# Solving the mixers' triangular systems on 64x64 diagonal blocks in two quadrants of TensorE

## The reference

```python
a = jnp.where(strict, jnp.einsum('bhntd,bhnsd->bhnts', kb, k) * decay, 0.0)
t_inv = lax.linalg.triangular_solve(a + eye, jnp.broadcast_to(eye, a.shape),
                                    left_side=True, lower=True, unit_diagonal=True)
u = jnp.einsum('bhnts,bhnsv->bhntv', t_inv, v * beta[..., None])
w = jnp.einsum('bhnts,bhnsd->bhntd', t_inv, kb * jnp.exp(gc)[..., None])
```

## Time and profile before

| | |
|---|---|
| median of 3 runs | 1672.39 us (1670.04 to 1673.32) |
| the profiled execution: its own time | 1669.19 us |
| its span, first to last instruction | 1667.4 us |
| TensorE products busy | 1611.3 us, 97% |
| VectorE busy | 1213.8 us, 73% |
| ScalarE busy | 986.9 us, 59% |
| mean granted clock of TensorE | 0.99 |

### The profile page before, as it was taken

How to read it: one execution, slowest core, us unless ns; L and a number is a source line. 1 busy time by engine, 2 the same in 40 slices (tenths; PEclk the granted TensorE clock), 3 DMA queues, 4 the chain that set the end, 5 groups by cost and what they waited for, 6 DMA issues and landing times.

```text
span 1667.4 us, 29382 instructions
## 1 busy us (share of the span) xinstructions
PE 1611.3 (97%) x12534; PEld 1523.0 (91%) x12534; DVE 1213.8 (73%) x1705; ACT 986.9 (59%) x1486; POOL 0.7 (0%) x6
## 2 busy tenths in 40 slices
PE   8999899999999999899999999989999999899998
PEld 7999899999989999899999988865999988699997
DVE  7889736777748789746777757666788758688864
ACT  7775555556546774565565543347677645567753
POOL 0000000000000000000000000000000000000000
PEclk9999999999999999999999999989999999999999
DMA  7422125455554412126555553620455544055551
GB/s 274 171 77 77 51 77 202 164 194 200 177 199 148 150 63 77 51 76 217 189 181 190 186 180 122 227 76 2 175 179 181 199 176 159 1 204 192 185 192 61
DMA packets 35843, 246.04 MB, mean 148 GB/s; under 512 B 4096, under 2 KB 4480, under 8 KB 6656
## 3 DMA queue, kind: packets, MB, share of 16 engines
q1 hardware_dynamic: 35712, 244.15, 41.2%
HBM read 243.09 MB, written 1.05 MB: 146 GB/s over the span
## 4 chain that ended last, share of the span: by engine, by line
PE 82%; DVE 10%; ACT 6%; DMA 1%; issue 1%; SPq 0%; DVEq 0%; ACTq 0%
PE PS L395 81%; DVE SB L1761 2%; DVE WL L1752 2%; DVE SB L1752 2%; ACT WH L1109 1%; ACT SB L1106 1%; DVE SA L1752 1%; DVE SB L2005 1%; ACT SA L1618 1%; ACT SB L1109 1%; DVE SB L2009 1%; DMA RAW<-w_in 0%; DVE SA L1919 0%; ACT SB L1690 0%; DVE SA L1761 0%
## 5 line engine op out<-in xcount | busy, mean ns | idle before, releaser
L395 PE MATMUL PS<-XH,WH 128*128 128x256 f32 (+1 forms) x2536 | 715.3, 282 | 8.9 <-DVE WL L1752 4.9
L395 PE MATMUL PS<-XL,WH 128*128 128x256 f32 (+1 forms) x2536 | 713.3, 281 | 0.0
L395 PE MATMUL PS<-XH,WL 128*128 128x256 f32 (+1 forms) x2536 | 712.8, 281 | 0.0
L1109 ACT CAST WH<-RAW 128x2048 fp32r<-128x2048 f32 (+1 forms) x229 | 427.0, 1865 | 398.3 <-PE PS L395 363.2
L1752 DVE TENSOR_TENSOR WL<-RAW,WH 128x2048 fp32r<-128x2048 f32 (+1 forms) x229 | 511.3, 2234 | 126.4 <-ACT WH L1109 122.4
L395 PEld LDWEIGHTS PS<-XH,WH 128*128 128x128 f32 (+1 forms) x2536 | 477.6, 188 | 14.6 <-issue 5.7
L395 PEld LDWEIGHTS PS<-XL,WH 128*128 128x128 f32 (+1 forms) x2536 | 475.7, 188 | 2.7 <-issue 1.9
L395 PEld LDWEIGHTS PS<-XH,WL 128*128 128x128 f32 (+1 forms) x2536 | 475.3, 187 | 0.4
L395 PE MATMUL PS<-INHL,WH 128*128 128x512 f32 (+1 forms) x1216 | 334.5, 344 | 1.2 <-DVE INHL L1752 1.2
L395 PE MATMUL PS<-INHL,WL 128*128 128x256 f32 x960 | 269.9, 281 | 0.0
L395 PEld LDWEIGHTS PS<-INHL,WH 128*128 128x128 f32 x1216 | 210.2, 188 | 29.2 <-ACT INHL L1109 1.5
(11 more groups left out here) (144 smaller groups left out, 1409.7 us busy)
## 6 DMA issues: line engine op xcount, KB each, us to landing
RAW<-w_in SPq DMA_DIRECT2D x51, 1024.0 KB, 4.8
RAW<-w_up SPq DMA_DIRECT2D x44, 1024.0 KB, 4.8
RAW<-f_in SPq DMA_DIRECT2D x44, 1024.0 KB, 4.7
RAW<-w_down SPq DMA_DIRECT2D x22, 1024.0 KB, 4.8
RAW<-f_out SPq DMA_DIRECT2D x22, 1024.0 KB, 4.7
RAW<-a_w_in SPq DMA_DIRECT2D x10, 1024.0 KB, 4.8
RAW<-w_out SPq DMA_DIRECT2D x8, 1024.0 KB, 4.8
RAW<-w_bdn SPq DMA_DIRECT2D x4, 1024.0 KB, 4.8
```

What stands on the lines that cost most here:

```text
L395: return e.matmul(out, l, r, start=start, stop=stop, skip_group_check=True)
L1109: e.copy(out, x).then_inc(*A.up(*key, of=of))
```

## The change

The 16 matrices of a mixer are kept for levels 1 to 5 as their diagonal blocks of 64x64 alone: XIc and XTc have 2 directions x 8 matrices of 64 columns, the upper block on partitions 0 to 63 (b = 0) and the lower one on partitions 64 to 127 (b = 1). A product of the two upper or the two lower blocks takes a quadrant of the array; b = 0 and b = 1 are issued in turn, into two banks of PSUM. The groups are now two (one for a direction) with 8 products for each b. ScalarE and VectorE read each bank on its 64 partitions, so there are still four copies of Y and four masked copies a level, and two transposes in place of four. Level 5 copies corners of 32x256. Level 6 computes the off-diagonal block alone (dn_y6, dn_z6: in the quadrants off the diagonal, one for each direction); ScalarE copies the diagonal blocks (blocks_out) and that block into XTF, full 128x128 matrices, whose fourth quarter GpSimd has set to zero. w_solve reads XTF.

The order changes too: Y of level 1 stands ahead of hg_diag on TensorE and ScalarE; ScalarE's exponential for step 0 stays first; on VectorE hg_mul(1) stands ahead of both placements of level 1; in all levels the placements of both directions stand together, between the first and the second HGRN step (TensorE: Z of both directions between hg_mm(n) and hg_mm(n + 1)).

The diff, cut to its core:

```diff
+        XIc, XTc = SB[:, 6144:7168], SB[:, 8192:9216]
+        XTF = [x.rearrange("p (m n) -> p m n", m=8) for x in (SA[:, 1024:2048], SB[:, 9216:10240])]
+        HALF = (slice(0, 64), slice(64, 128))
...
+                def dn_y(d, lv):
                     w.wait_ge(*V["at", st])
-                    side_placed(g4, lv - 1, 0)
-                    for h in range(4):
-                        last = mm(p[:, h * 128:h * 128 + 128], at_d(g4 // 2, g4 % 2)[:, h], XIv[:, g4, h], True, True)
-                    last.then_inc(*P.up("ps", st, "y", g4, lv))
-                    ps.give(st, "y", g4, lv)
...
+                    side_placed(d, lv - 1, 0)
+                    outs = [bank(st, "y", d, b, lv) for b in range(2)]
+                    for m in range(8):
+                        for b, p in enumerate(outs):
+                            last = mm(p[HALF[b], m * 64:m * 64 + 64], at_d(d, m // 4)[HALF[b], m % 4, HALF[b]], XIv[HALF[b], d, m], True, True)
+                            if m == 7:
+                                last.then_inc(*P.up("ps", st, "y", d, b, lv))
...
+                    for side in (0, 1) if lv == 5 else (0,):
+                        outs = [bank(st, "z", d, b, lv, side) for b in range(2)]
...
+                def dn_y6():
...
+                    for m in range(8):
+                        for d, p in enumerate(outs):
+                            last = mm(p[HALF[1 - d], m * 64:m * 64 + 64], at_d(d, m // 4)[HALF[d], m % 4, HALF[1 - d]],
+                                      XIv[HALF[d], d, m], True, True)
...
                 for lv in range(1, 7):
+                    if lv < 6:
+                        dn_y(0, lv)
+                        dn_y(1, lv)
+                    else:
+                        dn_y6()
                     if lv == 1:
                         hg_diag()
-                    for g4 in range(4):
-                        dn_y(g4, lv)
                     hg_mm(n)
...
```

ScalarE and VectorE:

```diff
-                        for g4 in range(4):
-                            cp(XTv[:, g4], ident.unsqueeze(1).to_broadcast([128, 4, 128]), "ident", st, g4)
+                        for b in range(2):
+                            cp(XTc[HALF[b]].rearrange("p (m n) -> p m n", m=16),
+                               ident[HALF[b], HALF[b]].unsqueeze(1).to_broadcast([64, 16, 64]), "ident", st)
...
+                def blocks_out():
+                    waits(*f2, G["zeros", st])
+                    for d in range(2):
+                        w.wait_ge(*A["placed", st, d, 5, 1])
+                        for b in range(2):
+                            cp(XTF[d][HALF[b], :, HALF[b]], XTv[HALF[b], d], "blocks out", st, d)
...
+                    for b in range(2):
+                        w.wait_ge(*P["ps", st, "z", d, b, lv, 0])
+                        cpred(XIv[HALF[b], d], block_mask(b, d, lv, 8), ps[st, "z", d, b, lv, 0][HALF[b], :].rearrange("p (m n) -> p m n", m=8),
+                              "placed", st, d, lv, 0, of=ps.out(st, "z", d, b, lv, 0))
+                    w.wait_ge(*V["placed", st, d, lv, 0])
+                    blocks_turned(XTc[:, x], XIc[:, x], "placed", st, d, lv, 1)
...
                         zproj(0)
+                        hg_mul(1)
                         dn_z(0, lv)
                         dn_z(1, lv)
-                        hg_mul(1)
-                        dn_z(2, lv)
-                        dn_z(3, lv)
...
+            for st in ("m0", "m1"):
...
+                    zeros(XTF[d][HALF[1 - d], :, HALF[d]], "zeros", st)
```

More of the change, by code:

```diff
@@ L610, in dn_z, with side_placed @@
[L610 to L621, removed]
+                def side_placed(d, lv, side):
+                    w.wait_ge(*V["placed", st, d, lv, side])
+                    w.wait_ge(*A["placed", st, d, lv, side])
@@ new lines, in dn_z6 @@
+                def dn_z6():
+                    for d in range(2):
+                        w.wait_ge(*A["y6", st, d])
+                        side_placed(d, 5, 1)
+                    outs = [bank(st, "z6", d) for d in range(2)]
+                    for m in range(8):
+                        for d, p in enumerate(outs):
+                            last = mm(p[HALF[d], m * 64:m * 64 + 64], YBv[d][HALF[1 - d], m], XTv[HALF[1 - d], d, m], True, True)
+                            if m == 7:
+                                last.then_inc(*P.up("ps", st, "z6", d))
+                    for d in range(2):
+                        ps.give(st, "z6", d)
@@ L1281, in placed, with unit @@
                         cp(o, x, *key, of=of)
[L1283 to L1288, removed]
-                    for side, M in ((0, XIv), (1, XTv)):
[L1290 to L1296, removed]
+                def unit(p):
+                    return p.rearrange("p (m n) -> p m n", m=8)
@@ new lines, in dn_y, with dn_y6 @@
+                def dn_y(d, lv):
+                    for b in range(2):
+                        w.wait_ge(*P["ps", st, "y", d, b, lv])
+                        cp(YBv[d][HALF[b]], unit(ps[st, "y", d, b, lv][HALF[b], :]), "y", st, d, lv, of=ps.out(st, "y", d, b, lv))
+                def dn_y6():
+                    for d in range(2):
+                        w.wait_ge(*P["ps", st, "y6", d])
+                        cp(YBv[d][HALF[1 - d]], unit(ps[st, "y6", d][HALF[1 - d], :]), "y6", st, d, of=ps.out(st, "y6", d))
@@ new lines, in dn_z @@
+                def dn_z(d, lv):
+                    for side, M in ((0, XIv), (1, XTv)):
+                        if lv < 5:
+                            A.note("placed", st, d, lv, side)
+                            continue
+                        for b in range(2):
+                            kind = d if side == 0 else 1 - d
+                            w.wait_ge(*P["ps", st, "z", d, b, lv, side])
+                            cp(corner(M[:, d], b, kind), corner(unit(ps[st, "z", d, b, lv, side]), b, kind), "placed", st, d, lv, side,
+                               of=ps.out(st, "z", d, b, lv, side))
@@ L1339, in mixer @@
                         hg_exp(0)
+                        w.wait_ge(*V["k sum", st])
+                    if lv < 6:
+                        dn_y(0, lv)
+                        dn_y(1, lv)
+                    else:
+                        dn_y6()
+                        blocks_out()
+                    if lv == 1:
                         hg_diag()
[L1341 to L1344, removed]
                         hg_exp(1)
@@ L1348, in mixer @@
                         hg_exp(n + 2)
[L1349 to L1350 removed]
+                    if lv < 6:
+                        dn_z(0, lv)
+                        dn_z(1, lv)
+                    else:
+                        dn_z6()
                     hg_mm(n + 1)
@@ L2019, in dn_z, with dn_first @@
[L2019 to L2032, removed]
+                def dn_first(d):
+                    waits(A["ident", st], V["at", st], A["k exp", st, 3])
+                    for b in range(2):
+                        for j in range(2):
+                            cpred(XTv[HALF[b], d, 4 * j:4 * j + 4], block_mask(b, 1 - d, 0, 4), at_d(d, j)[HALF[b], :, HALF[b]],
+                                  "placed", st, d, 0, 1)
+                    w.wait_ge(*V["placed", st, d, 0, 1])
+                    blocks_turned(XIc[:, d * 512:d * 512 + 512], XTc[:, d * 512:d * 512 + 512], "placed", st, d, 0, 0)
@@ new lines, in dn_z @@
+                def dn_z(d, lv):
+                    x = slice(d * 512, d * 512 + 512)
+                    if lv >= 5:
+                        for side in range(2):
+                            V.note("placed", st, d, lv, side)
+                        return
+                    for b in range(2):
+                        w.wait_ge(*P["ps", st, "z", d, b, lv, 0])
[3 more added lines that the diff above has]
+                    blocks_turned(XTc[:, x], XIc[:, x], "placed", st, d, lv, 1)
@@ L2082, in mixer @@
                 k_sum(3)
-                for g4 in range(1, 4):
-                    dn_first(g4)
+                dn_first(1)
                 def zproj(c):
```

86 lines of the change are left out of this document (52 added, 34 removed).

## The result

The change made the kernel slower: 1676.16 us (median of 20 runs, 1671.08 to 1679.01) against 1671.10 us (20 runs, 1668.87 to 1673.97), a ratio of 1.0028 with a 95% interval from 1.0021 to 1.0035. The forecast was 1667.0. The profiled execution took 1674.65 us, its span is 1672.9, its mean granted clock 0.978 (0.990 before).

The account below looks back on a forecast made before the run. TensorE (97% busy) was taken to bound the kernel, the solve's chain passing between TensorE and VectorE. A gain of 5.6 us a mixer less 2.9 for the clock, 5.4 in all, turned 1672.39 into 1667.0; range 1660.5 to 1673.0.

Parts of the forecast that it names:

- The clock takes back half: Levels 5 and 6: two of three new TensorE rests bring half clock, costing 2.9 us a mixer; net gain 2.7 a mixer.
- 3.4 as today: Level 5: TensorE's step 9 runs at half clock after the change too, taking 3.4 us as before.
- The rest of the sum: Solve, level by level before the clock's cost: gain 0 in level 1, 5.6 us a mixer at the end.
- VectorE's pieces ahead of step 9: Levels 1 to 4: VectorE sets the pace with 45.65 us of work, ending at 180.1 instead of 184.3, gain 4.2.
- Rival B: Levels 5 and 6: the clock holds through the new rests; gain 11.2 us, 1661.2; chance 0.20.
- TensorE's part: Solve products Y and Z: quadrant pairs at 0.060 us a pair of passes relieve TensorE of 20 us a mixer.
- rival C: Solve products: a pair of passes still costs 0.109 us; gain 0 to 1 a mixer, 1672; chance 0.22.
- VectorE's part: Levels 1 to 4: masked copies and transposes take 4.1 us a level instead of 5.6, 1.5 less.
- the two bounds of the copy: VectorE's masked copy of 64 partitions: 0.36 us (half) or 0.72 (like 128 partitions); the upper was taken.
- the remaining case of half price: VectorE's masked copies of half the partitions cost half, 16 x 0.3 us a mixer more; gain over 12; chance 0.05.
- the memsets of GpSimd: Four memsets in GpSimd's idle stretch cost nothing; if they slowed VectorE, 1 us each at most.
- Rival D: From step 9 on: half the array at work does not restore a fallen clock; 3.7 us a mixer slower, 1679.8; chance 0.08.

## Why the prediction was wrong

**The step that failed is "The clock takes back half".** It took two of three new rests, on the path, "for 1.5 each less what overlaps: 2.9 a mixer". Measured is 8.2 a mixer (16.4 over two mixers, by filling all rests). Its mechanism was right and stood there with the right sign; its size was off. The two numbers don't cover the same stretches: the prediction had step 9 at half clock in another term ("3.4 as today", 1.5 us), and filling all rests removes that one too. Like for like the prediction gave the clock 4.4 us a mixer for 8.2. Three things were missing in the term, each visible by the changed kernel beside the one with all rests filled:

- Level 1 has rests as well, 2.53, 1.29 and 2.27 us, and the term looked only at levels 5 and 6. The HGRN diagonal runs at half clock (3.03 us for 16 passes at 129.32), and step 1 comes 1.5 us later than with the rests filled (14.21 for 12.67 from the mark); 1.5 is still there at step 9.
- Step 9 had a half-clock stretch already and was costed "as today". But today's was hidden: taking it away gave the kernel before 0.25 us a mixer. After the change VectorE has no placements left to do beside it, and step 9 (1.7 us longer) and Z of level 5 (1.5) take the distance to 4.7 us at step 11.
- All the late rests fell, not two of three: 4.07 (forecast 3.7), 3.27 (2.9), 2.43 (3.1). Steps 13 and 15 at half clock add 1.7 and 1.6. The sum is 1.5 + 3.2 + 1.7 + 1.6 = 8.0 of the 8.06 in the table.

**The rest of the sum came out near, in part by luck.** The column with all rests filled and the forecast's differ by 1.1 us at step 9 (58.59 for 57.46) and by 0.3 to 0.6 the other way behind it. But the forecast's column has step 9 at half clock and the filled kernel's has not: from step 9 to Z of level 5 the forecast is 9.6 us, the filled kernel 8.1, the changed one 9.8. Two errors met there, VectorE's pieces ahead of step 9 that were 1.1 us too short, and 1.5 us of clock that the filled kernel doesn't pay. So the gain, 5.6 a mixer in the forecast, is 5.95 with all rests filled (96.48 less 90.53). Rival B, a clock that holds through the new rests, gave 1661.2 for 11.2; the filled kernel gained 11.9. B's number is near the value of the change without the clock, with the same luck in it.

**TensorE's part: right.** A pair of quadrant passes costs 0.058 us where 0.060 was assumed (32 passes take 1.15 us, 64 take 2.08). That is close to the lower of the two bounds, 0.055, and rival C, passes that do not shrink, is refuted. The 128 passes of Z in level 5 were forecast at 3.9 and take 3.95 at full clock.

**VectorE's part: right in kind, a little short.** Levels 2 and 3 together were put at 26.1 and take 25.48, VectorE busy for 24.9 of it. The timeline of VectorE at level 1 shows the pieces:

```profile
136.49 1.48 DVE L2076 COPY_PREDICATED SB<-MK,PS 64x512 f32<-64x512 uint8 x2
138.00 0.71 DVE L2080 STREAM_TRANSPOSE SB<-SB 128x512 f32<-128x512 f32 x1
138.74 1.51 DVE L2076 COPY_PREDICATED SB<-MK,PS 64x512 f32<-64x512 uint8 x2
```

Two copies and a transpose are 2.25 us (136.49 to 138.74), not 2.05, so these cost 0.4 a level more than assumed. Levels 2 and 3 came out shorter in spite of that; which pieces of levels 1 and 4 make up the 1.1 us that step 9 is late was not separated (0.3 of it is there at step 1). Groups by shape over the solve (busy us, mean ns) settle the two bounds of the copy:

```profile
L2076 DVE COPY_PREDICATED SB<-MK,PS 64x512 f32<-64x512 uint8 x16 | 11.7, 730 | 0.6 <-PE PS L406 0.2
...
L1152 ACT COPY SB<-PS 64x512 f32<-64x512 f32 x23 | 13.3, 579 | 1.3 <-PE PS L406 0.8
```

A masked copy of 64 partitions takes 0.730 us, one of 128 took 0.717; ScalarE's 0.579 and 0.582 for the two widths. The upper bound was the right one, and the remaining case of half price is refuted. The rule of the Trainium skill that the prediction weighed here (TensorEngine Tiling (Array Packing), Performance Considerations, that tiling leaves the emptying of PSUM as it was) agrees with the traces: halving those copies gave 10.4 us. The transposes are 10 for 20, as said, and the memsets of GpSimd, 1.04 us for two, lie under other work.

**Rival D** had the right side and the wrong mechanism. It said that half the array at work does not bring the clock back. It does. Z of level 5 consists of quadrant passes only; it starts at full clock, falls to half 0.55 us later, and is back at full from 196.25 on, with nothing but quadrant passes at work in between. Windows of the changed kernel:

```profile
192.84:196.25 3.41, 3.41 (x72) 3.41 (x68) 0.00 (x0) 3.02 (x7) 0.00 (x0) 0.50 0.51 214
196.25:197.72 1.47, 1.47 (x52) 1.40 (x49) 0.00 (x0) 0.80 (x3) 0.00 (x0) 1.00 0.00 0
```

What made the kernel slower is not that the clock stays down but that it falls five times.

**Where this left the chances.** The prediction gave slower 0.10 and a range up to 1673.0, made from rivals that each varied one thing. The clock term had a lower end (none of three, B) but no upper one: all rests, on the path, and level 1 with them. At the 1.5 us per stretch that it used, four new stretches are 6 us a mixer, 12 in all; against the gain of 11.2 that is no change, about 1673, the very end of the range given, which should have reached beyond it.

## What to carry to other kernels

When an edit makes TensorE's work shorter where another engine already has little to spare, list every rest that it opens or lengthens, in all stages that it touches, and price the clock for each on its own; what today's half-clock stretch costs is no price if today's is hidden behind another engine. Filling the rests with products that nobody reads is a cheap test and here also a cure, but fill all of them: with one filled, the fall can move to the next rest, as it did in one of two mixers here. A rest that kept its clock in one trace is no safe one. Work packed into quadrants should share a PSUM bank, so that one copy of all partitions empties it.

## What the runs showed of the hardware

- Granted clock: the level of 1.2 GHz began behind rests of 2.87 us (kernel before, step 9 filled), of 2.43 and 3.27 us (after), and after two rests of 2.53 and 1.29 close together; a rest of 1.8 us in the kernel before left it at 2.4 GHz. The length of the rest alone does not decide: the same 2.87 us ahead of the same group left the clock at 2.4 GHz in the second mixer (3.84 us for 5.46), 3.27 us ahead of step 13 did with level 1 filled (2.05 us in the second mixer), and 2.95 us ahead of Z of level 5 did in the kernel with one bank (3.95 us). What decides was not found.
- Two quadrants, rows and columns 0 to 63 and 64 to 127, wrote the two partition halves of one PSUM bank side by side in the kernels with one bank, at the same pace: levels 2 and 3 ran with TensorE full at 11.52 us and a clock of 1.00.
- The number of partitions did not enter the time of a copy: 0.730 and 0.717 us on VectorE, 0.579 and 0.582 on ScalarE, for 64 and 128 partitions of 512 elements.
